# A modulation vector by row sums in one VectorE instruction per 128 outputs, in a kernel bound by TensorE

## The reference, cut to what matters

```python
c_act = jax.nn.silu(c)
for l in range(DEPTH):
    mod = (c_act @ w_ada[l] + b_ada[l]).reshape(B, N_SUB, 3, D_MODEL)   # w_ada[l]: 1024 x 9216
    def norm_mod(h, j):
        shift = mod[:, j, 0][:, None, :]
        scale = mod[:, j, 1][:, None, :]
        return _rms(h) * g_norm[l, j] * (1.0 + scale) + shift
    def gate(j):
        return (1.0 + mod[:, j, 2])[:, None, :]
    x = x + 0.5 * gate(0) * _swiglu(norm_mod(x, 0), w_ffn_up[l, 0], w_ffn_down[l, 0])
    x = x + gate(1) * _mixer(norm_mod(x, 1), ...)
    x = x + 0.5 * gate(2) * _swiglu(norm_mod(x, 2), w_ffn_up[l, 1], w_ffn_down[l, 1])
```

## Time and profile before

| | us |
|---|---|
| median of three runs | 3699.4 (3698.81 to 3702.16) |
| profiled execution, its time | 3718.38 |
| profiled execution, its span | 3716.6 |
| PE busy | 3634.4 (98%) |
| DVE busy | 2023.8 (54%) |
| ACT busy | 1607.3 (43%) |
| mean granted clock of TensorE | 0.972 |

### The profile page before, as it was taken

One profiled execution on the slowest core, in us unless ns is written; L12 is line 12 of the kernel. 1 busy time (PEld: TensorE's weight loads), 2 busy tenths in 40 slices (PEclk: granted clock), 3 DMA queues, 4 the chain that ended last, 5 costly groups with the idle time before them and its releaser, 6 DMA issues.

```text
span 3716.6 us, 50808 instructions
## 1 busy us (share of the span) xinstructions
PE 3634.4 (98%) x20983; PEld 3055.5 (82%) x20983; DVE 2023.8 (54%) x3369; ACT 1607.3 (43%) x2496; POOL 203.4 (5%) x274
## 2 busy tenths in 40 slices
PE   9999999999999999999999999999999999889999
PEld 7887888888887888888888878888888887678888
DVE  7966477548765477545444556544443335554332
ACT  7447443326446544333222685322232226853221
POOL 1010100002020100010000100000000001000000
PEclk9979999999979999999999998999999999989999
DMA  3201144432201144443444211344422332112232
GB/s 122 69 24 41 58 153 150 145 130 81 69 19 40 58 158 149 148 129 122 151 144 145 75 46 53 135 148 145 139 97 97 97 92 70 40 46 97 97 100 87
DMA packets 108693, 368.26 MB, mean 99 GB/s; under 512 B 14128, under 2 KB 16560, under 8 KB 108464
## 3 DMA queue, kind: packets, MB, share of 16 engines
q1 hardware_dynamic: 108464, 365.02, 29.4%
HBM read 360.78 MB, written 4.19 MB: 98 GB/s over the span
## 4 chain that ended last, share of the span: by engine, by line
PE 86%; ACT 7%; DVE 6%; issue 1%; POOL 1%; DMA 0%; SPq 0%; DVEq 0%; ACTq 0%; POOLq 0%
PE bank L175 84%; ACT L398 3%; ACT tmp L190 1%; PE bank L259 1%; DVE wl L193 1%; PE bank L181 1%; DVE score L217 1%; ACT wh L190 1%; DVE ast L214 1%; ACT lr L190 0%; DVE tmp L196 0%; POOL x L193 0%; DVE dk L196 0%; DVE bA L193 0%; DVE dv L196 0%
## 5 line engine op out<-in xcount | busy, mean ns | idle before, releaser
L175 PE MATMUL bank<-hh,wh 128*128 128x512 f32 (+2 forms) x3424 | 1289.1, 376 | 15.4 <-ACT lg L190 7.2
L175 PE MATMUL bank<-hl,wh 128*128 128x512 f32 (+2 forms) x3424 | 1287.2, 376 | 0.0
L175 PE MATMUL bank<-hh,wl 128*128 128x512 f32 (+2 forms) x3424 | 1283.5, 375 | 0.7 <-DVE wl L193 0.7
L190 ACT ACTIVATE wh<-raw 128x1024 fp32r<-128x1024 f32 (+1 forms) x542 | 559.1, 1036 | 1427.0 <-PE bank L175 1420.7
L193 DVE TENSOR_TENSOR wl<-raw,wh 128x1024 fp32r<-128x1024 f32 (+1 forms) x542 | 650.9, 1204 | 788.1 <-ACT wh L190 787.7
L175 PEld LDWEIGHTS bank<-hh,wh 128*128 128x128 f32 (+1 forms) x3424 | 649.1, 190 | 133.4 <-issue 23.2
L175 PEld LDWEIGHTS bank<-hh,wl 128*128 128x128 f32 (+1 forms) x3424 | 648.7, 189 | 109.5 <-issue 2.6
L175 PEld LDWEIGHTS bank<-hl,wh 128*128 128x128 f32 (+1 forms) x3424 | 648.9, 190 | 107.6 <-issue 4.0
L175 PE MATMUL bank<-ah,wh 128*128 128x512 f32 (+1 forms) x1188 | 438.8, 369 | 0.0
L175 PE MATMUL bank<-ah,wl 128*128 128x512 f32 (+1 forms) x1188 | 438.5, 369 | 0.0
L175 PE MATMUL bank<-al,wh 128*128 128x512 f32 (+1 forms) x1188 | 438.3, 369 | 0.0
(11 more groups left out here) (371 smaller groups left out, 3734.5 us busy)
## 6 DMA issues: line engine op xcount, KB each, us to landing
raw<-in_up_dram SPq DMA_DIRECT2D x264, 512.0 KB, 3.3
raw<-in_ada_dram SPq DMA_DIRECT2D x144, 512.0 KB, 4.2
raw<-in_in_dram SPq DMA_DIRECT2D x88, 512.0 KB, 3.3
raw<-in_down_dram SPq DMA_DIRECT2D x96, 448.0 KB, 3.3
raw<-in_down_dram SPq DMA_DIRECT2D x48, 512.0 KB, 3.5
raw<-in_out_dram SPq DMA_DIRECT2D x32, 512.0 KB, 3.2
x<-in_x_dram SPq DMA_DIRECT2D x16, 256.0 KB, 4.9
raw<-in_in2v_dram SPq DMA_DIRECT2D x8, 512.0 KB, 3.6
```

The costliest lines, as they stand in the source:

```text
L175: s = self.put(lambda e: e.matmul(out, lhsT, rhs, **kw), records * max(records * n, 2 * m) / 2.4)
L190: return self.put(lambda e: e.activation(out, x, func, **kw), cost, tables)
```

## The change

Each of the 144 steps now works out 128 values completely, and on DVE alone. The weights `w_ada` are laid out transposed, so that a 512 KB piece holds 128 outputs in the partitions and their 1024 weights in the row. One `scalar_tensor_tensor` per piece multiplies the row by `crow`, a 128x1024 tile that holds silu(c) in every partition, writes the products back over the piece, and gives each row's sum through `accum_out` straight to a column of `mod`. The biases are added once per layer (128x72). No PE instruction is left in a step.

`crow` has to be made, since silu(c) lies in the partitions (`cact`, 128x8): `spread_condition` lets PE lay it out with eight float32 matmuls (`bank<-con,cact 128x128`) into bank 7, four at a time, and ACT copies each four to SBUF. The 4 KB per partition of `crow` lie where the mixers have `high` and `mod_sum`, so `crow` is made anew after a mixer: three times, before the FFNs of the first block's two layers and before the second FFN of the second block's first layer. (The first FFN there finds it still in place.) To make room, the fifth buffer of the FFN's turn `gv` becomes `acc`, which the norms use. The last step of a layer now also works out `dmod`, so that the loop in `run` asks for no step of its own between the blocks.

```diff
+        self.crow = self.place("crow", [P, 1024], F32, 229344 - 4096)
...
-        self.gv = Turn([... for i in range(5)])
+        self.gv = Turn([... for i in range(4)] + [self.acc])
...
+def spread_condition(mem):
+    q, done = mem.modulate, []
+    for n, b in enumerate((mem.banks[7], mem.banks[7])):
+        for k in range(4):
+            q.pe.wait_ge(mem.c_ready, mem.con_in, b.free)
+            m = q.pe.matmul(b.ap[:, P * k:P * k + P], mem.cact[:, 4 * n + k:4 * n + k + 1].to_broadcast([P, P]), mem.k("ident"), start=True, stop=True).then_inc(q.pe.sem, 1)
+        q.act.wait_ge(m, mem.mix_ready, mem.high.free, mem.mod_sum.free)
+        done.append(q.act.activation(mem.crow[:, 512 * n:512 * n + 512], b.ap[:, :], ACT.Copy).then_inc(q.act.sem, 1))
+        b.free = [done[-1]]
+    mem.crow_ready, mem.crow_used = done, []
...
-        for g in range(18):
-            a, s = mem.mod_sum, None
-            for k in range(4):
...
-                        s = q.dve.tensor_scalar(a.ap[:, :], x, w, None, ALU.mult).then_inc(q.dve.sem, 1)
...
-                        s = q.dve.scalar_tensor_tensor(a.ap[:, :], x, w, a.ap[:, :], ALU.mult, ALU.add).then_inc(q.dve.sem, 1)
-                r.free = [s]
-                if k == 3:
-                    b = mem.banks[5]
-                    for j in range(4):
-                        q.pe.wait_ge(s, mem.con_in, b.free)
-                        m = q.pe.matmul(b.ap[:, j:j + 1], a.ap[:, 128 * j:128 * j + 128], mem.k("ones", 1), start=True, stop=True).then_inc(q.pe.sem, 1)
...
+        for n in range(72):
+            r, w_ = mem.raw.next(), mem.weights
+            w_.sp.wait_ge(r.free)
+            landed = w_.sp.dma_start(r.ap[:, :], mem.A["ada"][l, n]).then_inc(r.sem, 16)
+            q.dve.wait_ge(landed, mem.crow_ready)
+            s = q.dve.scalar_tensor_tensor(r.ap[:, :], r.ap[:, :], 1.0, mem.crow[:, :], ALU.mult, ALU.mult, accum_out=mem.mod[:, l, n:n + 1]).then_inc(q.dve.sem, 1)
+            r.free = [s]
+            mem.crow_used.append(s)
+            if n < 71:
                 yield
+        q.dve.wait_ge(s)
+        columns.append(q.dve.tensor_tensor(mem.mod[:, l, :], mem.mod[:, l, :], mem.p2(l, "b_ada", 0, 72), ALU.add).then_inc(q.dve.sem, 1))
...
+        spread_condition(mem)
         normed(mem, lambda i: mem.p1(l, "ffn_pre", i))
         up_geglu(mem, l)
...
+                if j and not l:
+                    spread_condition(mem)
                 up_swiglu(mem, l, j // 2)
```

More of the change, by code:

```diff
@@ L193, in tensor_tensor, with scalar_tensor_tensor @@
         return self.vector(lambda e: e.tensor_tensor(out, a, b, op), width(out))
-    def scalar_tensor_tensor(self, out, a, scalar, b, op0, op1):
-        return self.vector(lambda e: e.scalar_tensor_tensor(out, a, scalar, b, op0, op1), width(out), 125.0)
+    def scalar_tensor_tensor(self, out, a, scalar, b, op0, op1, **kw):
+        return self.vector(lambda e: e.scalar_tensor_tensor(out, a, scalar, b, op0, op1, **kw), width(out), 185.0 if kw else 125.0)
     def tensor_scalar(self, out, a, s1, s2, op0, *op1):
@@ L592, in __init__ @@
         self.al = self.place("al", [P, NF, S], FR, at + NF * S * 4)
-        self.gv = Turn([Slot(self.place(f"gv{i}", [P, S], F32, at + 2 * NF * S * 4 + 2048 * i)) for i in range(5)])
+        self.gv = Turn([Slot(self.place(f"gv{i}", [P, S], F32, at + 2 * NF * S * 4 + 2048 * i)) for i in range(4)] + [self.acc])
         self.mod_sum = Slot(self.place("mod_sum", [P, S], F32, 229344 - 2048))
@@ L602, in __init__ @@
         self.ffn, self.modulate, self.output = self.lane("ffn"), self.lane("modulate"), self.lane("output")
-        self.x_ready = [None] * NT
+        self.x_ready, self.mix_ready = [None] * NT, []
         self.h_ready = [None] * NT
@@ L606, in __init__ @@
         self.mod_ready = [[None] * 3 for _ in range(DEPTH)]
-        self.due = 0
+        self.due, self.crow_used = 0, []
         self.r = [None, None]
@@ L1078, in modulation_steps @@
         columns = []
-        for g in range(18):
-            a, s = mem.mod_sum, None
-            for k in range(4):
[L1082 to L1089, removed]
-                        s = q.dve.tensor_scalar(a.ap[:, :], x, w, None, ALU.mult).then_inc(q.dve.sem, 1)
-                    else:
-                        q.dve.wait_ge(landed, s)
-                        s = q.dve.scalar_tensor_tensor(a.ap[:, :], x, w, a.ap[:, :], ALU.mult, ALU.add).then_inc(q.dve.sem, 1)
-                r.free = [s]
-                if k == 3:
-                    b = mem.banks[5]
-                    for j in range(4):
-                        q.pe.wait_ge(s, mem.con_in, b.free)
-                        m = q.pe.matmul(b.ap[:, j:j + 1], a.ap[:, 128 * j:128 * j + 128], mem.k("ones", 1), start=True, stop=True).then_inc(q.pe.sem, 1)
[L1100 to L1104, removed]
+        for n in range(72):
[7 more added lines that the diff above has]
+            if n < 71:
                 yield
+        q.dve.wait_ge(s)
+        columns.append(q.dve.tensor_tensor(mem.mod[:, l, :], mem.mod[:, l, :], mem.p2(l, "b_ada", 0, 72), ALU.add).then_inc(q.dve.sem, 1))
         for j in range(3):
@@ L1114, in modulation_steps @@
             mem.mod_ready[l][j] = [columns[-1], s, e]
+        yield
 def log1p(mem, q, out, e, w, z, wait):
@@ L1311, in mixer1 @@
     before = list(mem.x_ready)
+    mem.high.free, mem.mod_sum.free = list(mem.crow_used), list(mem.crow_used)
     x_free = normed(mem, lambda i: mem.p1(l, "mix_pre", i))
@@ L2534, in layout @@
         down1=tiles(ffn_w_down),
-        ada=np.ascontiguousarray(w_ada_2.reshape(2, 8, 128, 18, 512).transpose(0, 3, 2, 1, 4)),
+        ada=np.ascontiguousarray(w_ada_2.transpose(0, 2, 1).reshape(2, 72, 128, 1024)),
         up2=paired(w_ffn_up_2), down2=tiles(w_ffn_down_2), in2=tiles(w_in_2, cols2), in2f=moving(w_in_2[..., 2560:2564]),
```

## The result

| us | before | changed |
|---|---|---|
| first measurement, median | 3699.11 (4 executions) | 3663.41 (4 executions) |
| profiled execution | 3718.38 | 3663.6 |
| mean over all executions (before: without the first four) | 3708.2 (94, standard deviation 6.8) | 3665.0 (21, 7.8) |
| mean granted clock in them | 0.9758 | 0.9784 |

The ratio of the changed kernel to the one before, as recorded, is 0.9882, 95% interval 0.9862 to 0.9903; the two medians of the first measurement alone give 0.9903, its upper end. So it is faster by about 1.2%: 43 us by the means (3708.2 - 3665.0 = 43.2; with standard errors of 0.7 and 1.7, about plus or minus 4). The forecast was 30. The first three executions of the kernel before, 3698.8 to 3702.2, lay close together and still 8 us under the mean of the 94 that came after. The two first medians would have said 35.7.

A forecast was written before the change was run, and what follows sets the result against it. PE, busy without a gap in each FFN, was taken as the bound; -33.6 (column sums) + 1.8 + 1.8 (layouts) = -30.0 us, so 3699.4 - 30 = 3669 us, range 3656 to 3686.

The forecast's parts named there:

- Column sums, 36 x 0.934 = 33.6 us: First four FFNs: removing 36 groups of column sums from PE saves 33.6 us, all on the path.
- Layouts among products, 1.8 us: Start of the fourth FFN: eight silu(c) layout matmuls at 0.22 us, unhidden, add 1.8 us.
- In the norms, 1.8: Norms before block one's two FFNs: 16 layout matmuls add 1.8 us, half of the bounds 0 and 3.5.
- DVE, 0 on the path at either bound: FFNs: 144 new row-sum instructions, 1.23 to 2.47 us each, taken as 1.4, add nothing to the path.
- The last mixer is planned anew ... I allow 10 us either way and take 0: Last mixer, between fifth and sixth FFN: a new plan could shift time 10 us either way; counted as 0.
- The base, "the median of the runs shown is 3699.4": Whole kernel: the starting time 3699.4 us from which the forecast gain of 30 us was subtracted.
- A: Last mixer and norms: new plan loses 10 us (3679) or wins 10 us (3659); chance 0.20, half each side.
- B: FFNs: another wait, for transfers or `wl`, replaces the sums, so little is won, about 3695 us; chance 0.05.
- D: Norms: silu(c) layouts and copies cost 5.9 us instead of 1.8, giving 3673; chance 0.72 together with the forecast.
- C: First two FFNs: DVE becomes the bound and the kernel gets slower, about 3707 us; chance 0.03.
- A last mixer that holds over 310 or under 300 us: Last mixer: the sign named beforehand as showing that its new plan lost or won time.
- The half rate: DVE row sums: by a quoted rule, two non-bf16 SBUF sources make each about 2.5 us; forecast would stay.

The follow-up runs named there:

- e9: Kernel before, with the planner's clock model shifted 1650 ns at the last mixer, giving it the changed kernel's plan there: mean 3701.5 us, ratio 0.9983.
- e10: Changed kernel, with the planner's clock model shifted 300 ns at the last mixer, giving it the old plan there: mean 3675.6 us, ratio 0.9914.
- e2: Kernel before without the column sums and their wait (modulation values wrong), DVE products and transfers kept: mean 3671.3 us, ratio 0.9901.
- e16: Kernel before without its column sums, measured again with a second profile: mean 3671.1 us, ratio 0.9888.
- e14: Changed kernel, unchanged, measured again with a fourth profile: mean 3668.9 us, ratio 0.9879.

## Why the prediction fell short

The direction, the place and the main term were right. The size was not: 30 forecast, 43 measured. By the ratio, 0.9882 of 3699.4 is 3655.7 us, just under the range's low end of 3656; the median of the first executions, 3663.4, is inside.

- **Column sums, 36 x 0.934 = 33.6 us:** measured 33.5, from the four stretches. Right. The comparison of two FFNs that differ only in these instructions gave the price to a tenth.
- **Layouts among products, 1.8 us:** measured 1.73. Right. (They stand ahead of the fourth FFN's unbroken stretch, so that this holds 344.91 and not the 347 that was forecast.) **In the norms, 1.8:** no stretch shows it, and three times as many didn't lengthen the stretch after the first FFN either. Over-priced by up to 1.8.
- **DVE, 0 on the path at either bound:** right, up to three times the work. The price of the instruction was taken at 1.4; it lasts 1.22, and the next one on DVE starts 1.14 us after it.
- **The step that failed: "The last mixer is planned anew ... I allow 10 us either way and take 0", and the same for the norms.** Averaged over the profiles, the last mixer's stretch fell from 307.2 us (306.1, 306.5, 309.0) to 300.6 (299.5, 301.2, 300.4, 301.2), 6.6 us, which e9 and e10 pin on the plan. The norm between the blocks fell from 47.2 (46.7, 46.7, 48.3) to 44.3 (44.4, 44.4, 43.9, 44.4), 2.9 us; it too was planned in another order, but there the cause was not isolated. e2 and e16 have it as well (44.7 and 44.8), so it comes without the row sums. The 10 us bound for the last mixer, from two mixers with different plans, was sound, and the sign couldn't be read from the profile.
- **The base, "the median of the runs shown is 3699.4":** three executions were taken as the kernel's time. Their median lay 8.8 us under the mean of 94. The sum itself was made against the profiled execution, at 3718.4 one of the long ones.

The balance: 33.5 + 6.6 + 2.9 - 1.5 (the stretch ahead of the fourth FFN, 296.3 to 297.8, which holds the layouts) = 41.5 of 43.2 us. It leaves out two parts in which executions of one kernel differ among themselves: the stretch from the first to the second FFN (477.3 before, 474.9 changed, by the profiles) and what lies before the first FFN (464.7 and 463.4, e14's by the `con,stat` mark), 3.7 together. With them the sum is 45.2, which is the difference of the profiled executions' means (3709.1 - 3663.9). The 3.7 are within the scatter from one execution to the next.

Of the rivals, A came true in part, on its winning side. B and D didn't occur, nor did C; four times the DVE work made the kernel slower, but by filler and not by waits for DVE. "A last mixer that holds over 310 or under 300 us" was named as what would show A: it was 299.5 in the first profile, but 300.4 to 301.2 in the three others.

## What to carry to other kernels

Where one engine holds the end without a gap, two stages of the same kernel that differ only in the work at issue price that work better than any instruction's duration. An instruction that keeps the full engine for a tiny result (a 128x1 column sum costs PE as much as half a product of 128x512 in each of its records) is worth moving to an engine with room; test the room by multiplying the new work until it shows, and then look at what fills the gaps: here it was the planner's own filler, and PE had hardly waited for the engine under test. When a planner orders the code, an edit in one place is also a new draw for every plan behind it: exchange the plans before you credit the edit.

## What the runs showed of the hardware

- VectorE's multiply with a row sum reads two float32 tiles in SBUF at the rate of a plain subtraction of that size: 1217 ns for 1024 columns, against 1233. The half rate that the prediction quoted from the Trainium skill ("Vector Engine (DVE) Microarchitecture Reference", section "Points that are easy to get wrong") doesn't occur here; the measurement decides. That such an operation is two instructions (the Trainium skill, "VectorE: DVE Perf Modes", section "Two Vector instructions with no wait between them") the trace agrees with: 144 readouts of 82 ns, and the next instruction can start together with one (478.39).
- One program on one core, on four chips, spreads over 32 us from execution to execution (3689.6 to 3721.6 in 94; 6 to 7 us of standard deviation within a set), and the mean granted clock goes with it: 2.9 us for each 0.001. A span compared with another says something only beside its clock, or stretch by stretch.
